# Layer A: the sample's projection first in plain fp32, then the prompt's projection and the sample's attention in one block of static order

## The chip, the cores and the metric

The kernel runs on one core of one Trainium2 chip. TensorE multiplies matrices, VectorE (DVE), ScalarE (ACT) and GpSimd (POOL) do elementwise work, and SyncE (SP) issues most of the loads; DMA engines move data between HBM and the on-chip SBUF. Matmul results land in PSUM banks, from which DVE or ACT copies ("evacuates") them. Every engine runs its own queue of instructions in order, and semaphores tie the queues together. The metric is the device time of one execution in microseconds (us): 3773.86 us as the median of three runs (3769.08 to 3776.07).

## The reference

One step of a two-layer encoder trunk, on 1024 prompt rows (positions 0 to 1023) and on 8 running streams of 16 new rows each (the sample, 128 rows), which attend to 1024 cached keys and values per stream. D_MODEL is 1024, all in fp32. Cut to layer A, which the change touches:

```python
hn = rmsnorm(h, norm_attn[l])
qkv = hn @ w_qkv_a[i]                                # 1024 x 3072
q, k, v = jnp.split(qkv, [A_QK, 2 * A_QK], axis=-1)  # 1024 columns each
q = rope(q.reshape(b, t, 2 * A_HEADS, A_HEAD_DIM), q_pos)
k = rope(k.reshape(b, t, 2 * A_HEADS, A_HEAD_DIM), q_pos)
k_all = concatenate([c_ak, k]);  v_all = concatenate([c_av, v])   # sample only
# diff_attend: two softmax maps per head, 8 heads, values of 128 columns
s = einsum('bqhmd,bkhmd->bhmqk', q, k) * A_HEAD_DIM ** -0.5
p = softmax(where(mask, s, NEG));  w = p[:, :, 0] - lam * p[:, :, 1]
o = einsum('bhqk,bkhe->bqhe', w, v)
h = h + (rmsnorm(o, subln_a) * 0.8) @ w_o_a          # then the MLP, then layer B
```

Outputs are the trunk's rows and the new keys and values of both layers, for prompt and sample.

## The kernel before, in words

The program is a chain of blocks that end in a barrier of all engines: `project_phase` "qkv" (prompt and sample rows together), `prompt_attention` "pa", `decode_attention` "da" (the sample's), `post_phase` "m" (output projection and MLP), and then the same for layer B.

`project_phase` works in 6 pieces of 512 columns (two for Q, two for K, two for V). The weights of a piece come in 4 parts of 512 KB (L201). A float32 product is made of three matmuls in the faster fp32r format (`product`, L144 to L146): every operand is split into a high part (a rounded copy, made by ACT: L438 for weights, L443 for rows) and the rest (`lo`: L240 on POOL for weights, L334 on DVE for rows). A unit is one piece for one row block of 128: 8 times 3 matmuls into a PSUM bank. Nine row blocks (8 prompt, 1 sample) times 6 pieces are 54 units. High and low weights are held for two pieces, so that the next piece is ready when the last ends. DVE evacuates each unit: for Q and K with the rotation, four instructions (L366, L368, L373, L376), for V with one (L360), and ACT's queue issues the store (L459).

`decode_attention` takes the 8 streams one after another. A stream b has 9 steps t, one for each tile of 128 keys (8 cached, one new). In a step TensorE transposes key tile t+1 (`keys`, L1502, 8 transposes into the two banks kb0 and kb1), which ACT (bank 0, L1673) and DVE (bank 1, L1612) evacuate to `kT`; it multiplies tile t with the queries (`scores`, L1520); and for the stream before it works through the probabilities: transposes (`probs`, L1538) and `values` (L1554). ACT makes the exponentials of stream b-1 in steps 0 and 1 of stream b (L1688). At the end, `select` (L1573) gathers the heads' rows. In step 0 TensorE must transpose two key tiles, 0 and 1, into the same two banks, and tile 1 waits until the copies of tile 0 are done. Scores and transposed probabilities have two PSUM banks each; key and value tiles have rings of 4 buffers in SBUF, loaded by SP (L1420, L1425).

The program's waits are on semaphores named in the code; what an engine does next is fixed by the order in which the code writes it. The residual rows `h` are loaded by the qkv block (L205 to L220) and stay in SBUF; `post_phase` adds the output projection to them in `out_add` (L843), after loading attention rows (L569) and weights (L564).

## Time and profile before

| what | value |
|---|---|
| median of three runs | 3773.86 us |
| the profiled execution's own time | 3774.97 us |
| its span, first to last instruction | 3773.3 us |
| mean granted TensorE clock | 0.962 |
| block qkv, from the start to the first load of pa | 0 to 333.4 us |
| block pa, to the first load of da | to 624.3 us |
| block da, to the first load of post_phase | to 855.3 us |
| TensorE busy, whole span | 91% |

All durations below come from the profiled execution. In a table of stretches, a row gives the stretch and its length, then for TensorE (PE), its weight loads (PEld), DVE, ACT and POOL the busy us and the count of instructions in brackets, then the granted TensorE clock as a share of full speed (1.00 is 2.4 GHz, 0.50 is 1.2 GHz), the share of time that the DMA engines were busy, and GB/s. In a timeline, a row gives start, length, engine, line, operation, output<-inputs and shapes; the brackets give how long the engine had been idle before and who ended that. A fp32 matmul is recorded as two rows of weights and two of matmul; an fp32r matmul or a transpose as one.

### The profile page before, as it was taken

The numbers are of one execution on the slowest core, as the hardware profiler recorded it, in microseconds if no ns is written. First come the engines' busy times: TensorE is split into PE (matmuls) and PEld (weight loads), VectorE is DVE, ScalarE is ACT, GpSimd is POOL, SyncE is SP. The second block draws the span as 40 slices with busy tenths as digits, with TensorE's granted clock in tenths as the row PEclk, the third lists the DMA queues.
The fourth block names the chain that finished last, engine by engine and source line by source line (L and its number), as shares of the span: only waits on it lengthen the run. The fifth ranks groups of instructions, "written<-read, shape, count | busy, mean of one in ns | idle before, by whom it ended". The sixth has DMA issues, their size and how long they took to land. (4 is left out here: it accounts for less than half of the span.)

```text
span 3773.3 us, 59284 instructions
## 1 busy us (share of the span) xinstructions
PE 3437.6 (91%) x22922; PEld 2965.5 (79%) x22922; DVE 1697.3 (45%) x2822; ACT 1075.7 (29%) x2054; POOL 478.4 (13%) x188
## 2 busy tenths in 40 slices
PE   7998887887999999999699978868978999999998
PEld 6886776766899999998588867755657899999997
DVE  5423886545444444444312166643432444444445
ACT  3002665333321111112200056642322222221112
POOL 2220000002111111111112100000002111111110
PEclk9998999998999999999889989988988999999999
DMA  4224443973011111110212143427763111111111
GB/s 149 92 85 90 91 100 126 335 285 124 23 45 44 44 44 42 36 44 12 71 59 93 59 100 79 90 57 239 279 214 113 34 45 44 35 43 44 44 50 51
DMA packets 286683, 344.89 MB, mean 91 GB/s; under 512 B 157312, under 2 KB 206496, under 8 KB 286560
## 3 DMA queue, kind: packets, MB, share of 16 engines
q1 hardware_dynamic: 266448, 303.98, 26.1%
q10 hardware_dynamic: 17824, 31.02, 2.3%
q0 software_dynamic: 2304, 8.39, 0.7%
q8 instruction: 76, 1.25, 0.1%
q14 instruction: 31, 0.25, 0.0%
HBM read 299.36 MB, written 43.98 MB: 91 GB/s over the span
## 5 line engine op out<-in xcount | busy, mean ns | idle before, releaser
L879 DVE SCALAR_TENSOR_TENSOR h_rows<-m_dn,m_factor,h_rows 128x512 f32<-128x512 f32 x576 | 429.2, 751 | 311.6 <-PE m_dn L146 311.6
L144 PE MATMUL m_dn<-m_wa,m_wb 128*128 128x512 f32 x1152 | 449.3, 390 | 0.4
L146 PE MATMUL m_dn<-m_wa,m_wb 128*128 128x512 f32 x1152 | 449.0, 390 | 0.0
L145 PE MATMUL m_dn<-m_wa,m_wb 128*128 128x512 f32 x1152 | 448.7, 390 | 0.0
L863 DVE TENSOR_TENSOR m_rows<-m_rows 128x384 f32<-128x384 f32 x192 | 165.5, 862 | 455.2 <-ACT m_rows L754 455.2
L144 PE MATMUL m_up<-b_xt_hi,m_wa 128*128 128x384 f32 x768 | 258.3, 336 | 7.4 <-DVE m_wb L869 4.5
L144 PE MATMUL m_up<-c_xt_hi,m_wa 128*128 128x384 f32 x768 | 257.7, 336 | 7.4 <-DVE m_wb L869 4.5
L145 PE MATMUL m_up<-b_xt_lo,m_wa 128*128 128x384 f32 x768 | 257.8, 336 | 0.0
L146 PE MATMUL m_up<-b_xt_hi,m_wa 128*128 128x384 f32 x768 | 257.7, 336 | 0.0
L146 PE MATMUL m_up<-c_xt_hi,m_wa 128*128 128x384 f32 x768 | 257.5, 335 | 0.0
L145 PE MATMUL m_up<-c_xt_lo,m_wa 128*128 128x384 f32 x768 | 257.3, 335 | 0.0
L144 PEld LDWEIGHTS m_dn<-m_wa,m_wb 128*128 128x128 f32 x1152 | 216.3, 188 | 46.0 <-DVE h_rows L879 2.1
L146 PEld LDWEIGHTS m_dn<-m_wa,m_wb 128*128 128x128 f32 x1152 | 216.2, 188 | 45.2
L145 PEld LDWEIGHTS m_dn<-m_wa,m_wb 128*128 128x128 f32 x1152 | 216.3, 188 | 44.0
L608 POOL TENSOR_TENSOR m_wa<-m_up_raw,m_wa 128x2048 fp32r<-128x2048 f32 x32 | 148.2, 4632 | 744.1 <-ACT m_wa L744 744.1
L749 ACT ACTIVATE m_wa<-m_dn_raw 128x2048 fp32r<-128x2048 f32 x32 | 61.4, 1918 | 632.3 <-PE m_dn L146 632.3
L610 POOL TENSOR_TENSOR m_wa<-m_dn_raw,m_wa 128x2048 fp32r<-128x2048 f32 x32 | 147.2, 4598 | 643.4 <-ACT m_wa L749 643.4
L754 ACT ACTIVATE m_rows<-m_up 128x384 f32<-128x384 f32 x192 | 94.4, 492 | 411.9 <-PE m_up L146 411.9
L144 PE MATMUL kv_acc<-kv_w_hi,b_xt_hi 128*128 128x512 f32 x432 | 173.6, 402 | 24.1 <-POOL kv_w_lo L240 24.1
L144 PE MATMUL qkv_acc<-qkv_w_hi,a_xt_hi 128*128 128x512 f32 x432 | 169.7, 393 | 10.6 <-POOL qkv_w_lo L240 10.6
L146 PE MATMUL kv_acc<-kv_w_hi,b_xt_lo 128*128 128x512 f32 x432 | 172.5, 399 | 0.0
L145 PE MATMUL kv_acc<-kv_w_lo,b_xt_hi 128*128 128x512 f32 x432 | 172.4, 399 | 0.0
(315 smaller groups left out, 6843.5 us busy)
## 6 DMA issues: line engine op xcount, KB each, us to landing
da_k_tiles<-in_cache_a_k SPq DMA_DIRECT2D x64, 512.0 KB, 6.0
da_v_tiles<-in_cache_a_v SPq DMA_DIRECT2D x64, 512.0 KB, 5.4
m_up_raw<-in_w_up SPq DMA_DIRECT2D x32, 1024.0 KB, 5.3
m_dn_raw<-in_w_down SPq DMA_DIRECT2D x32, 1024.0 KB, 4.9
db_k_tiles<-in_cache_b_k SPq DMA_DIRECT2D x64, 512.0 KB, 4.8
db_v_tiles<-in_cache_b_v SPq DMA_DIRECT2D x64, 512.0 KB, 4.5
qkv_w_raw<-in_w_qkv_a SPq DMA_DIRECT2D x24, 512.0 KB, 3.9
m_rows<-o_scratch SPq DMA_DIRECT2D x18, 512.0 KB, 4.0
```

The lines of the kernel that those rows point to most:

```text
L144: pe.matmul(out, lh, rh, start=start, stop=False)
L145: pe.matmul(out, lh, rl, start=False, stop=False)
L146: return pe.matmul(out, ll, rh, start=False, stop=stop)
L608: pool.tensor_tensor(up_lo, up_raw[:], up_hi.bitcast(F32), ALU.subtract).then_inc(s_ul, 1)
L610: pool.tensor_tensor(dn_lo, dn_raw[:], dn_hi.bitcast(F32), ALU.subtract).then_inc(s_dl, 1)
L749: act.activation(dn_hi, dn_raw[:], ACT.Copy).then_inc(s_dh, 1)
L754: act.activation(rl[:, n % 2, :], ups[n % 3][:, 0:GW], ACT.Relu).then_inc(s_ue, 1)
L863: dve.tensor_tensor(rq[:, n % 2, :], rl[:, n % 2, :], rl[:, n % 2, :], ALU.mult).then_inc(s_rq, 1)
L879: dve.scalar_tensor_tensor(hc, dns[n % 3], r2[:, r:r + 1], hc, ALU.mult, ALU.add).then_inc(s_de, 1)
```

## The change

`project_phase` "qkv" and `decode_attention` "da" of layer A are replaced by one block, `project_decode` (tag "da"), and `prompt_attention` runs after it.

First the sample: its 128 rows are transposed and multiplied, unsplit, with the raw fp32 weights of each piece (`sample_unit`, 6 pieces of 8 matmuls), while the prompt's rows are transposed and split. All weights are thus loaded twice, once here and once for the prompt. Then the prompt's 48 units (6 pieces, 8 row blocks) and the decode steps follow one list, `ORDER`, which all engines walk: for each piece four pairs of (convert a quarter of the weights; one decode step), then eight units, each followed by one or two decode steps. The converted weights have room for one piece only. The low part of the weights is now made by DVE with a gain multiply, and the high part by ACT, in calls of 512 columns. The banks for scores and for transposed probabilities are single, the value ring has 3 buffers, and `select` of stream b-2 is in steps 0 and 1 of stream b.

Behind each unit of the first piece and unit 0 of the second stand two steps, behind every other unit one.

The residual rows are no longer loaded by the first block; `post_phase` loads them from the inputs (`load_h`) when `first` is given.

```diff
+def project_decode(nc, core, tag, pieces, gain_src, x, table, lams, k_cache, v_cache, o_rows):
...
+        raw = sb("w_raw", [P, PARTS, KP, HALF])
+        whi, wlo = (sb(f"w_{v}", [P, KT, HALF], F32R) for v in ("hi", "lo"))
...
+        def schedule():
+
+
+
+            steps = [(b, t) for b in range(NB + 1) for t in range(CT + 1)]
+            order, s, units = [], 0, NP * PT
+            for i in range(NP):
+                for j in range(PARTS):
+                    order.append(("weights", i, j))
+                    order.append(("step",) + steps[s])
+                    s += 1
+                for r in range(PT):
+                    order.append(("unit", i, r))
+                    left = (NP - 1 - i) * PARTS
+                    n = -(-(len(steps) - s - left) // (units - i * PT - r))
+                    for _ in range(n):
+                        if s < len(steps):
+                            order.append(("step",) + steps[s])
+                            s += 1
+            return order
...
+            def load_part(n):
+                if n >= PARTS:
+                    if n - PARTS < NS:
+                        sp.wait_ge(s_sw, n - PARTS + 1)
+                    else:
+                        sp.wait_ge(s_wlo, n - PARTS - NS + 1)
+                w, c0 = pieces[n // PARTS % NP][0:2]
+                sp.dma_start(raw[:, n % PARTS], w[:, c0:c0 + HALF].rearrange("(k p) n -> p k n", p=P)[
+                    :, k0_of(n):k0_of(n) + KP, :]).then_inc(s_raw[n % PARTS], 16)
+
+            def load_row(q):
+                if q >= 2:
+                    sp.wait_ge(s_tp, 2 if q == 2 else ROW_EVENT[q - 3] + 2)
+                    sp.wait_ge(s_sq, q - 1)
+                src = x[1] if q == 0 else x[0][(q - 1) * P:q * P, :]
+                sp.dma_start(stage[q % 2], src).then_inc(s_row[q % 2], 16)
...
+                for j in range(PARTS):
+                    load_part(PARTS * (i + 1) + j)
+            load_row(PT)
+            for n in range(KR):
+                load_k(n)
+            for n in range(VR):
+                load_v(n)
+            k, v = KR, VR
+            for kind, a, c in ORDER:
+                if kind == "weights":
+                    if a + 1 < NP:
+                        load_part(NS + PARTS * (a + 1) + c)
+                elif kind == "step":
+                    if c < CT and a < NB:
+                        load_k(k)
+                        k += 1
+                    if a >= 1:
+                        for y in VALUES[c]:
+                            if y < CT:
+                                load_v(v)
+                                v += 1
...
+            def sample_unit(i):
+                if i == 0:
+                    for g in range(2):
+                        pe.wait_ge(s_tf[g], 1)
+                at_least(pe, s_ev, i - 1)
+                for j in range(PARTS):
+                    n = PARTS * i + j
+                    pe.wait_ge(s_raw[j], 16 * (i + 1))
+                    for k in range(KP):
+                        ins = pe.matmul(acc[i % 2][:], xs[:, KP * j + k, :], raw[:, j, k, :],
+                                        start=j == 0 and k == 0, stop=j == PARTS - 1 and k == KP - 1)
+                    ins.then_inc(s_sw, 1)
+
+            def unit(i, r):
+                n = i * PT + r
+                pe.wait_ge(s_ev, NP + n - 1)
+                if i == 0:
+                    e = ROW_EVENT[r] + 1
+                    pe.wait_ge(s_tf[e % 2], e // 2 + 1)
+                    pe.wait_ge(s_tf[1 - e % 2], (e - 1) // 2 + 1)
+                for k in range(KT):
+                    if r == 0 and k % KP == 0:
+                        pe.wait_ge(s_wlo, PARTS * i + k // KP + 1)
+                    lhs = [v[:, k, r * P:(r + 1) * P] for v in (xt_hi, xt_lo)]
+                    ins = product(pe, acc[n % 2][:], lhs, (whi[:, k, :], wlo[:, k, :]), k == 0, k == KT - 1)
+                ins.then_inc(s_mm, 1)
...
+            def step(b, t):
+                if b < NB:
+                    if t == 0:
+                        keys(b, 0)
+                    if t + 1 < CT:
+                        keys(b, t + 1)
+                    scores(b, t)
+                if b >= 2 and t < 2:
+                    select(b - 2, t)
+                if b >= 1:
+                    for v in VALUES[t]:
+                        values(b - 1, v)
+                    for pair in PROBS[t]:
+                        probs(b - 1, pair)
...
+        def evacuation(eng, copy, half):
+
+
+            def keys(b, t):
+                n = b * CT + t
+                eng.wait_ge(s_ktr, 2 * n + half + 1)
+                at_least(eng, s_qk, n - 1)
+                copy(kT[:, t % 2, 4 * half:4 * half + 4, :], KB[half][:]).then_inc(s_ke[half], 1)
...
+            def weight_high(i, j):
+                act.wait_ge(s_raw[j], 16 * (NP + i + 1))
+                at_least(act, s_mm, PT * i)
+                for k in range(KP * j, KP * j + KP):
+                    ins = act.activation(whi[:, k, :], raw[:, j, k % KP, :], ACT.Copy, scale=gcol[:, k:k + 1])
+                ins.then_inc(s_whi, 1)
+
+            def store(i, r):
+                n = i * PT + r
+                dst, d0 = pieces[i][3]
+                act.wait_ge(s_ev, NP + n + 1)
+                act.dma_start(dst[r * P:(r + 1) * P, d0:d0 + HALF], ob[:, n % 2, :]).then_inc(s_st[n % 2], 16)
+
+            def exp(b, g):
+                act.wait_ge(s_nm, b + 1)
+                if b == 0:
+                    act.wait_ge(s_tp, EVENTS)
+                    act.wait_ge(s_sq, RT)
+                at_least(act, s_ptr, 5 * b)
+                at_least(act, s_cf, 2 * b)
+                act.activation(pr[:, g, :], sc[:, g, :], ACT.Exp, bias=nmx[:, g:g + 1],
+                               accum_out=ds[:, g:g + 1]).then_inc(s_e, 1)
...
+            def step(b, t):
+                if b >= 1 and t < 2:
+                    exp(b - 1, t)
+                if b < NB:
+                    if t == 0:
+                        keys(b, 0)
+                    if t + 1 < CT:
+                        keys(b, t + 1)
+                    if t % 2 == 1 or t == CT:
+                        scores(b, t // 2)
+                if b >= 2 and t == 1:
+                    selected(b - 2, 1)
+                    rows_store(b - 2)
+                if b >= 1:
+                    for pair in PROBS[t]:
+                        probs(b - 1, pair)
...
+            for kind, a, c in ORDER:
+                if kind == "weights":
+                    weight_high(a, c)
+                elif kind == "unit":
+                    store(a, c)
+                else:
+                    step(a, c)
...
+            def unit_out(i, r):
+                n = i * PT + r
+                dve.wait_ge(s_mm, n + 1)
+                dve.wait_ge(s_ev, NP + n)
+                if i == 0:
+                    dve.wait_ge(s_rt, r + 2)
+                dve.wait_ge(s_st[n % 2], 16 * (1 + n // 2))
+                rows_out(acc[n % 2][:], r + 1, pieces[i][2], ob[:, n % 2, :], core.cos_sin(r))
+
+            def weight_low(i, j):
+                dve.wait_ge(s_whi, PARTS * i + j + 1)
+                for k in range(KP * j, KP * j + KP):
+                    ins = dve.scalar_tensor_tensor(wlo[:, k, :], raw[:, j, k % KP, :], gcol[:, k:k + 1],
+                                                   whi[:, k, :].bitcast(F32), ALU.mult, ALU.subtract)
+                ins.then_inc(s_wlo, 1)
...
+                factor(i + 1)
+            for kind, a, c in ORDER:
+                if kind == "weights":
+                    weight_low(a, c)
+                elif kind == "unit":
+                    unit_out(a, c)
+                else:
...
+            def load_h(r):
+                if first:
+                    sp.dma_start(h[:, r, :], rows_of(*first[:2], r)).then_inc(s_hr0[r], 16)
...
+                load_h(r - 1)
                 if r + 2 < 2 * PARTS:
                     load_w(r + 2)
+            load_h(RT - 1)
+            if first:
+                for y in range(2):
...
+                if first and p == 0:
+                    dve.wait_ge(s_hr0[r], 16)
...
-        with ExitStack() as rows:
-            core.normed_rows(rows, "a")
-            project_phase(nc, core, "qkv",
-                          [(wa, c, "rope", (*qd, c), 0) for c in (0, HALF)]
-                          + [(wa, D + c, "rope", (kv["ak_p"], kv["ak_s"], c), 0) for c in (0, HALF)]
-                          + [(wa, 2 * D + c, "store", (kv["av_p"], kv["av_s"], c), 0) for c in (0, HALF)],
-                          gains, first=(a["norm_attn"][0, :], a["const"], lams))
+        project_decode(nc, core, "da",
+                       [(wa, c, True, (qd[0], c), (None, c)) for c in (0, HALF)]
+                       + [(wa, D + c, True, (kv["ak_p"], c), (kv["ak_s"], c)) for c in (0, HALF)]
+                       + [(wa, 2 * D + c, False, (kv["av_p"], c), (kv["av_s"], c)) for c in (0, HALF)],
+                       a["norm_attn"][0, :], (xp, xs), a["const"], lams, cak, cav, ao)
+        core.clear_semaphores()
         prompt_attention(nc, core, "pa", False, q, kv["ak_p"], kv["av_p"], None, None, ao)
-        decode_attention(nc, core, "da", False, q[SEQ:ROWS, :], kv["ak_s"], kv["av_s"], cak, cav, None, None, None, ao)
         core.clear_semaphores()
+        core.residual_rows(ctx)
         with ExitStack() as rows:
             core.normed_rows(rows, "b")
             post_phase(nc, core, "m0", ao, a["w_o_a"].rearrange("n d e -> (n d) e"), a["subln_a"][0, :],
-                       a["w_up"][0], a["w_down"][0], a["norm_mlp"][0, :])
+                       a["w_up"][0], a["w_down"][0], a["norm_mlp"][0, :], (xp, xs, gains))
```

How the change orders TensorE at the start of the program: before, the fp32r units begin right behind the first transposes (`turn` is the bank of transposed rows, `acc` a unit's bank).

```order
L251 MATMUL qkv_turn<-const_sb,qkv_xn 128x128 x16
L144 MATMUL qkv_acc<-qkv_w_hi,a_xt_hi 128x512
L145 MATMUL qkv_acc<-qkv_w_lo,a_xt_hi 128x512
L146 MATMUL qkv_acc<-qkv_w_hi,a_xt_lo 128x512
L144 MATMUL qkv_acc<-qkv_w_hi,a_xt_hi 128x512
```

After, on the same engine at the same place (`xs_T` holds the sample's rows, `probs` is the buffer in which raw rows are staged, `out_rows` a finished piece of the sample):

```order
L702 MATMUL da_kb<-const_sb,da_probs 128x128 x8
L723 MATMUL da_acc<-da_w_raw,da_xs_T 128x512 x8
L702 MATMUL da_kb<-const_sb,da_probs 128x128 x8
L723 MATMUL da_acc<-da_w_raw,da_xs_T 128x512 x8
L702 MATMUL da_kb<-const_sb,da_out_rows 128x128 x4
L702 MATMUL da_kb<-const_sb,da_probs 128x128 x8
L723 MATMUL da_acc<-da_w_raw,da_xs_T 128x512 x8
```

Six such fp32 groups, with all row transposes, now stand ahead of the first decode step and the first prompt unit.

Step 0 of a stream on ACT, before: the copy of key tile 0 stands ahead of the exponential (line 1688), the copy of tile 1 behind it. The rows without a tile are register work and waits.

```order
L1673 ACTIVATE da_kT<-da_kb 128x512
L1686 ISA
L1687 ISA
L1688 ACTIVATE da_probs,da_sum<-da_scores,da_neg_max 128x1152
L1610 REGISTER_ALU
L1611 REGISTER_ALU
L1673 ACTIVATE da_kT<-da_kb 128x512
```

After, step 0 of stream 3, behind unit 2 of the second piece, on ACT (`q_scratch<-da_out_rows` is the store of a unit, which waits until DVE has evacuated it):

```order
L926 DMA q_scratch<-da_out_rows 128x512
L935 ACTIVATE da_probs,da_sum<-da_scores,da_neg_max 128x1152
L882 ACTIVATE da_kT<-da_kb 128x512 x2
L926 DMA q_scratch<-da_out_rows 128x512
L935 ACTIVATE da_probs,da_sum<-da_scores,da_neg_max 128x1152
```

The unit's store and the exponential now stand ahead of both key copies of the step.

The boundary between the second and the third piece on DVE. Before, DVE had no weights to convert there, only unit after unit:

```order
L366 SCALAR_TENSOR_TENSOR qkv_times_cos<-qkv_acc,row_factor,const_sb 128x512
L368 SCALAR_TENSOR_TENSOR qkv_times_sin<-qkv_acc,row_factor,const_sb 128x512
L373 TENSOR_TENSOR qkv_out_rows<-qkv_times_cos,qkv_times_sin 128x8x32
L376 TENSOR_TENSOR qkv_out_rows<-qkv_times_cos,qkv_times_sin 128x8x32
L366 SCALAR_TENSOR_TENSOR qkv_times_cos<-qkv_acc,row_factor,const_sb 128x512
```

After, on DVE (line 1050 ends the evacuation of the second piece's last unit, `w_lo` are the weights' low parts, `kT` the key copies):

```order
L1050 TENSOR_TENSOR da_out_rows<-da_out_rows,da_times_sin 128x8x32
L848 COPY da_kT<-da_kb 128x512
L1100 TENSOR_REDUCE da_max<-da_scores 128x2
L1075 SCALAR_TENSOR_TENSOR da_w_lo<-da_w_raw,da_gain_column,da_w_hi 128x512 x2
L848 COPY da_kT<-da_kb 128x512
L870 COPY da_probs_T<-da_pb 128x256
L1075 SCALAR_TENSOR_TENSOR da_w_lo<-da_w_raw,da_gain_column,da_w_hi 128x512 x2
L861 COPY da_scores<-da_sb 128x2x128 x2
L1100 TENSOR_REDUCE da_max<-da_scores 128x2
L1075 SCALAR_TENSOR_TENSOR da_w_lo<-da_w_raw,da_gain_column,da_w_hi 128x512 x2
```

Between two units there now stand the weights' low parts, each ahead of the next step's copies.

## Rows read from the trace of the kernel before

**Rows 1.** The page's head.
```profile
span 3773.3 us, 59284 instructions
```
**Rows 2.** Table of stretches, cut at the three blocks of layer A.
```profile
0.00:333.40 333.40, 306.41 (x1368) 253.49 (x1368) 122.66 (x215) 49.16 (x73) 58.82 (x29) 1.00 0.29 100
333.40:624.30 290.90, 238.61 (x1632) 210.18 (x1632) 226.91 (x448) 175.80 (x416) 7.75 (x10) 0.93 0.42 87
624.30:855.30 231.00, 190.60 (x3136) 149.21 (x3136) 103.72 (x192) 89.18 (x180) 4.94 (x17) 0.95 0.83 300
```
**Rows 3.** Stretches: start-up, the units behind it, and seven streams of da.
```profile
0.00:27.00 27.00, 3.91 (x16) 3.14 (x16) 7.14 (x11) 11.23 (x15) 10.86 (x8) 1.00 0.71 253
27.00:331.00 304.00, 302.50 (x1352) 250.35 (x1352) 114.84 (x200) 36.69 (x57) 47.95 (x20) 1.00 0.25 86
...
660.00:848.00 188.00, 162.34 (x2790) 127.98 (x2792) 88.70 (x165) 73.96 (x150) 3.48 (x12) 0.97 0.86 312
```
**Rows 4.** Stretch of the middle of da.
```profile
660.00:748.00 88.00, 79.31 (x1412) 63.69 (x1414) 44.87 (x82) 36.37 (x74) 1.74 (x6) 1.00 0.91 333
```
**Rows 5.** Timeline of TensorE, the first unit: slow matmuls, then fast ones.
```profile
27.64 0.63 PE L145 MATMUL qkv_acc<-qkv_w_lo,a_xt_hi 128*128 128x512 f32 x1
28.06 0.63 PE L146 MATMUL qkv_acc<-qkv_w_hi,a_xt_lo 128*128 128x512 f32 x1
...
32.03 0.39 PE L145 MATMUL qkv_acc<-qkv_w_lo,a_xt_hi 128*128 128x512 f32 x1
32.26 0.40 PE L146 MATMUL qkv_acc<-qkv_w_hi,a_xt_lo 128*128 128x512 f32 x1
```
**Rows 6.** Timeline of da, step 0 of a stream, and its select.
```profile
726.55 1.64 PEld L1573 LDWEIGHTS da_pb<-da_o_diag,const_sb 128*16 128x16 f32 x16 [1.18 <-ACT da_o_diag L1680]
...
728.40 0.85 PEld L1502 LDWEIGHTS da_kb<-const_sb,da_k_tiles 128*128 128x128 f32 x8 [0.21 <-issue]
...
730.09 0.60 ACT L1673 ACTIVATE da_kT<-da_kb 128x512 f32<-128x512 f32 x1 [0.91 <-PE da_kb L1502]
730.59 1.25 ACT L1688 ACTIVATE da_probs<-da_scores,da_neg_max 128x1152 f32<-128x1152 f32 x1
730.74 0.86 PEld L1502 LDWEIGHTS da_kb<-const_sb,da_k_tiles 128*128 128x128 f32 x8 [1.48 <-ACT da_kT L1673]
```
**Rows 7.** Timeline of da, TensorE: a step with values, scores to scores.
```profile
742.66 0.38 PEld L1520 LDWEIGHTS da_sb<-da_kT,da_q_diag 128*32 128x32 f32 x16 [0.17 <-issue]
...
745.56 0.38 PEld L1520 LDWEIGHTS da_sb<-da_kT,da_q_diag 128*32 128x32 f32 x16 [0.17 <-issue]
```
**Rows 8.** A unit's evacuation on DVE: ns minimum, median and maximum, and when.
```profile
L366 DVE SCALAR_TENSOR_TENSOR qkv_times_cos<-qkv_acc,row_factor,const_sb x36: 750/751/752, 34.8 to 231.7; 128x512 f32<-128x512 f32 x36
L368 DVE SCALAR_TENSOR_TENSOR qkv_times_sin<-qkv_acc,row_factor,const_sb x36: 741/743/743, 35.4 to 232.4; 128x512 f32<-128x512 f32 x36
L360 DVE TENSOR_SCALAR qkv_out_rows<-qkv_acc,row_factor x18: 750/751/751, 237.1 to 329.6; 128x512 f32<-128x512 f32 x18
```
**Rows 9.** The same evacuation's third instruction.
```profile
L373 DVE TENSOR_TENSOR qkv_out_rows<-qkv_times_cos,qkv_times_sin x36: 424/425/1149, 36.2 to 233.1; 128x256 f32<-128x256 f32 x36
```
**Rows 10.** Groups of 660 to 848 us: key copies, busy us, mean ns, idle before.
```profile
L1612 DVE COPY da_kT<-da_kb 128x512 f32<-128x512 f32 x52 | 36.0, 691 | 37.4 <-PE da_kb L1502 37.4
...
L1673 ACT ACTIVATE da_kT<-da_kb 128x512 f32<-128x512 f32 x52 | 30.9, 594 | 32.6 <-PE da_kb L1502 32.4
```
**Rows 11.** The page's DMA issues: KB each, median us to landing.
```profile
da_k_tiles<-in_cache_a_k SPq DMA_DIRECT2D x64, 512.0 KB, 6.0
da_v_tiles<-in_cache_a_v SPq DMA_DIRECT2D x64, 512.0 KB, 5.4
...
qkv_w_raw<-in_w_qkv_a SPq DMA_DIRECT2D x24, 512.0 KB, 3.9
```
**Rows 12.** Timeline: the first transposes of da, and its last store.
```profile
632.04 3.59 PE L1482 MATMUL da_kb<-const_sb,da_new_rows 128*128 128x128 f32 x16 [13.27 <-DMA da_new_rows<-out_ak_s]
...
851.98 0.33 ACTq L1702 DMA_DIRECT2D o_scratch<-da_o_out  x1
```

418 lines of the change are left out of this document (415 added, 3 removed).

## The prediction

> **What bounds the kernel now.** I read the page's head first (the whole span) [rows 1], then the table of stretches cut at the barriers of layer A. The three blocks take 333.4, 290.9 and 231.0 us [rows 2]. Only the first and the third are rewritten, 564.4 us together. In the first, TensorE is busy for 302.5 of 304.0 us behind a start-up of 27 us [rows 3]: it is bound by TensorE's pace. Two fp32r matmuls start 0.23 us apart at full clock [rows 5]. The 54 units and the transposes fill 27 to 329.6 us; with 72 transposes at 0.11 (0.85 us for eight [rows 6]), which is 8, and 2 us for the slow start, a unit is (302.6 - 10)/54 = 5.42, and I use 5.44 us. In the third, TensorE is busy for 162.3 of the 188 us of seven streams, 26.9 us a stream, with the DMA engines at 0.86 [rows 3]. The timeline tells which steps wait. A step with values goes from scores to scores in 2.90 us [rows 7], filled to the 0.2 us turns between kinds of matmul: it can't be hidden, only moved. Step 0 waits: TensorE transposes key tile 0 at 728.40 and tile 1 only at 730.74, 1.48 us of it on ACT's copy [rows 6]. The idle part is 25.7/7 = 3.7 us a stream; by adding the turns back differently it is up to 4.9. So a stream is 22.0 to 23.2 us of TensorE work, I take 22.5, and da is 180 us of work in 231. The 51 us of rest (13.3 us before the first transposes [rows 12], the last stream's values alone, the 3.7 a stream) are all that interleaving can recover.
>
> **The change part by part** (us; durations from the profiled execution, 3774.97 us, which is 1.1 above the median of the runs).
>
> *Removed:* 54 units and both blocks: 564.4.
>
> *Sample phase.* An fp32 matmul of 128 columns takes 1.64/8 = 0.205 (sixteen weight rows) [rows 6], so one of 512 columns four times that, 0.82 to 0.85, and a piece 8 x 0.85 = 6.8, against 5.44 as a unit. Start: in the first 27 us loads move 253 GB/s [rows 3], so the sample rows are there at about 6.5, turned and scaled at 10, and piece 0 runs for its first 4 us at the slow level (0.42 between matmuls [rows 5]): it ends at 19. Each further piece has 6.8, eight transposes (0.9), four for the new Q and K (0.45), and the wait for ACT to free their bank (0.6 copy [rows 10], and its turn): 9.1. Pieces 1 to 4 and the last: 66.
>
> *Transition.* The last prompt row's load waits in SP's queue behind all sample weights and lands 8 later; transpose, high part, square and root take until +12. Then four pairs of weight conversion and step run in lockstep: DVE has 2 x 0.75 for the low part [rows 8], 0.69 for its key copy [rows 10], and maxima, some 3.3 a pair, and TensorE needs that copy before the next pair. Unit 0 starts at 66 + 23.5, plus 2.5 for the slow clock behind such gaps: 92. The row for a TensorE without work before 27 us [rows 3] is the bound from below (start of units at 75), 105 the one above.
>
> *Units and steps.* 48 x 5.44 = 261. Steps 180, less the 7 that lie in the transition: 173.
>
> *Step 0 of streams 1 to 7.* Behind a rotated unit, ACT first waits for the evacuation, 0.2 + 0.75 + 0.74 + 0.42 + 0.42 = 2.55 [rows 8, 9], issues the store (3.0), makes the exponential (1.25 + 0.19, to 4.4) and only then copies key tile 0 (5.0). TensorE had finished its transpose at 0.9 and waits 4.1 for the bank; behind that wait stand its scores, the select and the next unit. Behind an unrotated unit it is 2.5. Seven times: 24. Before, that wait was 1.48 [rows 6] and is in the 231.
>
> *Two steps behind a unit* (nine times): the second one's transposes need ACT's copy, at 3.5 for the same reason, and find TensorE ready after 1.4 (no values), 2.5 or 2.9: 0.6 to 2.1 each, 3.5 with an exponential: 12.
>
> *Piece boundaries.* DVE has the last unit's 2.35, five steps' copies and four low parts of 1.5; TensorE has five steps of 22.5/9, 12.5, and can start the next unit after about 16.5. Five times 4: 20. Before, two pieces of weights were held and this was nothing. If all steps there were light it could be 2, with exponentials 7.
>
> *Value tiles.* A tile takes 5.4 to land [rows 11]; a ring of three with two tiles used in a step of 2.9 starves where such steps follow each other without a unit between (four boundaries and three double steps): 1.5 to 3 each, partly under DVE's wait: 10, bounds 0 and 25.
>
> *Tail.* Last outputs, select, copy and store: 8. Afterwards one more barrier, 1; residual rows reloaded in a stretch with spare DMA, queued behind the attention rows they could delay: 1.
>
> Sum: 92 + 261 + 173 + 24 + 12 + 20 + 10 + 8 = 600, and 2 behind it; before 564.4. The difference is +37, on 3774.97 it is 3812, and against the median 3811. I take 3810.
>
> A row and a rule on the clock: in the middle of da, two fifths of whose TensorE work is transposes (82 a stream, 0.11 each [rows 6], of 22.5), the granted clock is 1.00, the level of 2.4 GHz, after unbroken work before it [rows 4]. The Trainium skill (TensorE: Matmul & The Clock Gate, Part 4: PE-mode transpose) says that transposes do not engage the full clock, as they don't count as busy in the same way. By that rule the sample phase and the steps would slow down in the new block; by the row they don't, and the sum has nothing for it.
>
> **The rivals.**
>
> *A. TensorE's waits are covered, and it gets faster.* For it: between two units every copy has 5.44 us to finish, ACT and DVE are busy for 74 and 89 of 188 us in da [rows 3], and key loads run three steps ahead. If sample phase and transition stay as computed and the waits (24 + 12 + 20 + 10) come to 15 in all, the block is 549 and the time 3775 - 15 + 2 = 3762; with a start of units at 75, 3745. Against it: the list fixes that store and exponential stand ahead of the copies.
>
> *B. The sample phase is bound by loads.* A loop moves four weight parts and a row, 2.6 MB; at 9.1 us that is 288 GB/s. For it: the start-up moved 253 [rows 3], at which a loop is 10.4 and the phase 7 longer: 3818. At a load's landing of 6 us [rows 11] behind its issue, the margin is only half a us. Against it: 333 GB/s were moved with tiles of the same 512 KB [rows 4]. The Trainium skill (DMA: Bandwidth & Descriptors, Bandwidth) asks for DMAs of at least 1 MiB for 75% of peak; its rule would make parts of 512 KB the bound of this phase. The row with several such tiles in flight speaks against it here.
>
> *C. The single banks and the short value ring decide.* All 20 or so heavy steps without a unit between take 4.3 instead of 2.9 (a ring of three per 5.4 + 0.9), and boundaries cost 8: 3810 + 28 = 3838. For it: the boundaries behind pieces 2 and 4 fall into value steps. Against it: landing is faster (3.9 [rows 11]) with less traffic.
>
> *D. It cancels:* gain of the interleaving and price of the sample phase within 7 us: 3774. For it: both are some 50 us, and my sum is a small difference.
>
> **How the numbers follow.** Forecast (3792 to 3828) 0.45, A 0.20, B 0.14, C 0.13, D 0.08. A difference below 0.2%, 7.5 us, can't be told from none. Faster comes from A: 0.20; same from D and the edge of A: 0.09; slower from the rest: 0.71. The forecast's own range is 3792 to 3828; to leave out no more than 0.2, with half of A inside and C up to its price, it becomes 3760 to 3842.
>
> **What would show it.** The first fp32r matmul of a unit at 85 to 100 us (below 80 the sample phase or the transition is oversized); fp32 matmul rows for the sample about 0.43 us apart; the block's end at 590 to 612; at each step 0, TensorE's transposes of tile 1 waiting 4 us on ACT's copy, and the ACT row of the exponential ahead of it; at piece boundaries about 16 us without an fp32r matmul; TensorE's busy time in the block about 440. The forecast is wrong if those waits are under 20 us together, if the units are spread (a unit over 5.6), or if the block of the prompt's attention changes from 291, which I hold constant.

## The result and the profile after

The changed kernel takes 3835.27 us (median of four, 3834.61 to 3838.08), the kernel before 3773.24 us beside it: a ratio of 1.016 with a 95% interval of 1.0148 to 1.0172. It is slower by 62 us, 25 more than the forecast of 3810. That is inside the stated range of 3760 to 3842, but 7 us outside the forecast's own 3792 to 3828. The profiled execution took 3834.74 us. First the page's head and the table of stretches of the changed kernel, in the columns of [rows 2]. The cuts are the end of the sample's pieces, the first prompt unit, the first load of the prompt's attention (pa) and that of the post phase:

```profile
span 3832.8 us, 58469 instructions
```
```profile
0.00:66.00 66.00, 54.43 (x169) 27.72 (x170) 21.62 (x52) 22.27 (x40) 1.28 (x7) 1.00 0.88 297
66.00:90.20 24.20, 13.86 (x120) 10.19 (x119) 12.56 (x24) 13.79 (x28) 0.00 (x0) 0.72 0.88 318
90.20:621.60 531.40, 462.38 (x4172) 367.20 (x4168) 206.97 (x372) 108.38 (x210) 5.30 (x14) 0.94 0.47 161
621.60:913.30 291.70, 237.24 (x1632) 210.09 (x1632) 226.73 (x448) 175.82 (x416) 7.76 (x10) 0.94 0.40 87
```

The new block ends at 621.6; the two it replaces took 564.4 [rows 2], so 57.2 are lost inside it. The prompt's attention takes 291.7 instead of 290.9, and all behind it 1.5 more (2919.5 us of the span against 2918.0). That is 59.5, the whole difference of the spans [rows 1]. Nothing went wrong elsewhere.

The third row is the one to read. From the first unit to the end, TensorE has 462.4 us of work and is idle for 69.0, and the granted clock is 0.94. The gaps and the clock go together, as will be seen.

The start came as forecast. TensorE in the sample phase (start, length, line): a piece of eight fp32 matmuls, recorded as 16 rows 0.43 apart, takes 7.0, and the pieces follow each other at 8.7 (30.84, 39.56). Then the last prompt row's transposes wait 5.6 for its load:

```profile
30.84 7.11 PE L723 MATMUL da_acc<-da_w_raw,da_xs_T 128*128 128x512 f32 x16 [1.17 <-DMA da_w_raw<-in_w_qkv_a]
...
39.56 7.03 PE L723 MATMUL da_acc<-da_w_raw,da_xs_T 128*128 128x512 f32 x16
...
72.63 1.97 PE L702 MATMUL da_kb<-const_sb,da_probs 128*128 128x128 f32 x8 [5.58 <-DMA da_probs<-in_x_prompt]
```

What TensorE waits for behind the first unit (us in total, times, longest), changed kernel:

```profile
PE da_kb L749 <- ACT da_kT L882: 37.2, 15, 4.4
PE da_ob L793 <- DMA da_v_tiles<-in_cache_a_v: 14.8, 9, 4.6
PE da_kb L749 <- DVE da_kT L848: 3.2, 4, 1.2
```

The largest is the step-0 wait, which [rows 6] show at 1.48. The timeline of one of them, behind a rotated unit of the fourth piece (step 0 of stream 6, with the exponentials of stream 5):

```profile
432.60 1.03 PE L749 MATMUL da_kb<-const_sb,da_k_tiles 128*128 128x128 f32 x8
...
435.16 0.34 ACTq L926 DMA_DIRECT2D out_ak_p<-da_out_rows  x1
435.62 1.25 ACT L935 ACTIVATE da_probs<-da_scores,da_neg_max 128x1152 f32<-128x1152 f32 x1 [6.16 <-DVE da_out_rows L1050]
...
436.88 0.58 ACT L882 ACTIVATE da_kT<-da_kb 128x512 f32<-128x512 f32 x1
...
437.60 1.94 PE L749 MATMUL da_kb<-const_sb,da_k_tiles 128*128 128x128 f32 x8 [3.96 <-ACT da_kT L882]
...
439.47 1.08 PE L764 MATMUL da_sb<-da_kT,da_q_diag 128*32 128x128 f32 x16
```

Read it from the right: TensorE finished tile 0's transposes at 433.6 and gets the bank back at 437.6. ACT had been idle for 6.16 us, in its queue behind DVE's rotation, because the unit's store stands ahead of the step; then store, exponential, and only then the copy. And the eight transposes behind the wait take 1.94 instead of 1.03, the sixteen score matmuls 1.08 instead of 0.64: the clock fell to 1.2 GHz in the gap, as the row of the stretch behind it shows (0.50). A wait of 4 costs over 5.

```profile
437.60:442.10 4.50, 4.50 (x32) 3.33 (x32) 0.69 (x1) 0.60 (x1) 0.00 (x0) 0.50 0.31 108
```

Key and value tiles land about as long behind their issue as before, weight parts 1.1 later [rows 11]; the weights are converted in calls of 719 ns on ACT:

```profile
da_k_tiles<-in_cache_a_k SPq DMA_DIRECT2D x64, 512.0 KB, 5.4
da_v_tiles<-in_cache_a_v SPq DMA_DIRECT2D x64, 512.0 KB, 5.5
...
da_w_raw<-in_w_qkv_a SPq DMA_DIRECT2D x48, 512.0 KB, 5.0
```
```profile
L919 ACT ACTIVATE da_w_hi<-da_w_raw,da_gain_column 128x512 fp32r<-128x512 f32 x40 | 26.4, 719 | 0.9 <-ACT da_xs_T L882 0.9
```

### The profile page after: what moved, and what is told of

It is laid out like the page before. It is cut to its first block and busy times, and to the rows that moved or that the text cites. A ratio compares the mean times of both kernels' runs of the same rounds, so it can differ in the third digit from the quotient of the medians.

```text
span 3832.8 us, 58469 instructions
## 1 busy us (share of the span) xinstructions
PE 3470.3 (91%) x22874; PEld 2968.3 (77%) x22874; DVE 1711.1 (45%) x2861; ACT 1081.6 (28%) x2078; POOL 421.3 (11%) x164
## 5 line engine op out<-in xcount | busy, mean ns | idle before, releaser
L363 DVE TENSOR_SCALAR kv_out_rows<-kv_acc,row_factor 128x512 f32<-128x512 f32 x54 | 40.5, 750 | 269.6 <-PE kv_acc L149 269.6
```

The lines of the kernel that those rows point to most:

```text
L363: dve.tensor_scalar(o, src_, rstd[:, r:r + 1], None, ALU.mult).then_inc(s_ev, 1)
```

## The experiments

Twelve kernels, all made from the changed one. Each is timed against the kernel before on its own chip, where the latter's median was 3774.7 to 3776.5 (3773.2 beside the changed kernel); differences of 1 to 3 us between two kernels of the table can come from that alone. "Stretch" is from the first prompt unit to the first load of pa; idle is its length less TensorE's busy time.

| run | median us | ratio to before (95%) | stretch | busy | idle |
|---|---|---|---|---|---|
| changed kernel | 3835.3 | 1.0148 to 1.0172 | 531.4 | 462.3 | 69.0 |
| e_actorder | 3805.6 | 1.0064 to 1.0091 | 499.2 | 451.7 | 47.5 |
| e_allorder | 3802.2 | 1.0055 to 1.0083 | 496.4 | 453.0 | 43.5 |
| e_doubles_late | 3827.2 | 1.0121 to 1.0152 | 520.0 | 457.0 | 63.0 |
| e_sequential | 3845.8 | 1.0165 to 1.0197 | - | - | - |
| e_order_ring | 3795.2 | 1.0038 to 1.0062 | 489.8 | 453.9 | 36.0 |
| e_lowpool | 3836.8 | 1.0142 to 1.0181 | 526.6 | 460.3 | 66.4 |
| e_best | 3796.9 | 1.0039 to 1.0065 | 486.0 | 449.6 | 36.4 |
| e_flush | 3779.8 | 1.0007 to 1.0024 | 471.8 | 441.8 | 30.1 |
| e_two | 3771.6 | 0.9986 to 1.0004 | 466.5 | 446.1 | 20.5 |
| e_none | 3775.9 | 0.9995 to 1.0012 | 467.0 | 443.0 | 23.9 |
| e_single_last | 3769.2 | 0.9972 to 0.9990 | 464.5 | 444.4 | 20.2 |
| e_stage | 3769.7 | 0.9979 to 0.9997 | 463.0 | 443.4 | 19.6 |

**e_actorder.**

```diff
@@ ScalarE
             def step(b, t):
+                if b < NB and t == 0:
+                    keys(b, 0)
                 if b >= 1 and t < 2:
                     exp(b - 1, t)
                 if b < NB:
-                    if t == 0:
-                        keys(b, 0)
...
+            waiting = []
             for kind, a, c in ORDER:
+                if kind != "step" and waiting:
+                    store(*waiting.pop())
...
-                    store(a, c)
+                    waiting.append((a, c))
```

> ScalarE only: in step 0 of a sequence the copy of key tile 0 stands ahead of the previous sequence's exponential, and the store of a prompt unit stands behind the steps that follow the unit. Theory (the order on ScalarE holds TensorE at step 0): of the 37.2 us that TensorE waits for a key copy of ScalarE, about half goes, since VectorE's own scores and unit copy come at nearly the same time; the block ends 10 to 20 us earlier, 3815 to 3825 us. Rival 1 (single banks of kb, sb, pb and the short ring of value tiles decide): within 4 us of the changed kernel, 3831 to 3839. Rival 2 (the slow clock behind each gap is the price): gaps get shorter, so the loss at the half clock falls as well and the gain is above 20 us, under 3815.

Measured: 30 us less, more than the theory's 10 to 20 and under 3815, as rival 2 said. The same place in its timeline, and its stretch:

```profile
410.70 1.03 PE L749 MATMUL da_kb<-const_sb,da_k_tiles 128*128 128x128 f32 x8
...
411.33 0.60 ACT L882 ACTIVATE da_kT<-da_kb 128x512 f32<-128x512 f32 x1 [5.03 <-PE da_kb L749]
...
411.83 1.25 ACT L935 ACTIVATE da_probs<-da_scores,da_neg_max 128x1152 f32<-128x1152 f32 x1
...
413.88 0.66 PE L749 MATMUL da_kb<-const_sb,da_k_tiles 128*128 128x128 f32 x4 [1.18 <-DVE da_kT L848]
414.47 0.64 PE L764 MATMUL da_sb<-da_kT,da_q_diag 128*32 128x128 f32 x16
```
```profile
88.77:587.99 499.22, 451.73 (x4172) 359.00 (x4168) 205.74 (x372) 110.52 (x210) 5.33 (x14) 0.97 0.51 171
```

The copy now stands ahead of the exponential and doesn't wait for the store, and what is late next is DVE's copy behind the rotation. From the first transpose to the scores it is 3.8 us against 6.9. The stretch is 32.2 shorter: 21.5 of it is idle time and 10.6 is busy time of the same 4172 recorded matmuls, which ran at a clock of 0.97 and not 0.94. So both explanations hold, two thirds to one third. The store was moved behind every unit, and not only where a step 0 follows, so the 32.2 spread: 14.0 come at the four steps 0 between units of a piece, 6.5 at the doubles, 4.8 at the boundaries, 3.2 in the units themselves and 3.7 behind the last unit.

**e_allorder.** As e_actorder, with the same `waiting` list around `unit_out` on DVE.

> The same, and on VectorE the rotation and copy of a unit's output stands behind the steps as well. Theory: both halves of a key tile are now copied before anything else is done at step 0 and behind a unit; waits at steps 0 and at doubles (34 us above the plain steps) fall to under 10, so 3800 to 3812 us. Rival 1 (single banks, ring): 3829 to 3839. Rival 3 (the unit's bank comes free too late, since acc is only double): the units that follow a double step wait for acc, and the time is that of e_actorder or up to 10 us more.

Measured: 3802, within the theory's interval, but only 3 less than e_actorder, which the intervals do not separate, and where some 14 had been expected between them. Its waits:

```profile
PE da_kb L749 <- ACT da_kT L882: 15.4, 10, 4.9
PE da_ob L793 <- DMA da_v_tiles<-in_cache_a_v: 14.7, 9, 4.3
```

The wait on ACT's copy, 8.2 in e_actorder, is back at 15.4, longest 4.9. The doubles of piece 0 gained (the gaps between its units fell from 35.0 to 29.2), while boundaries 3 and 4 grew from 18.7 and 25.0 to 23.7 and 28.0. Why is seen in e_flush.

**e_doubles_late.** `n` in the list is rounded down instead of up, so that two-step places come last.

> The two-step places stand at the last eight units instead of the first ones. Theory: the eight doubles of the first piece cost 20 us above plain steps, because the evacuations of two steps and a unit's rotation meet there; the last piece's units are value units that are not rotated, so the same doubles are cheaper by 8 to 12 us there, 3823 to 3828 us. Rival (the key stream bounds the doubles, one key tile in 3.2 us at most from the pool of queues): the same time, 3831 to 3839, since the stream's waits move with them.

Measured: 8 less, 3827, as the theory said. The waits on ACT's copy fell from 37.2 to 30.9, those for value tiles rose from 14.8 to 19.0:

```profile
PE da_kb L749 <- ACT da_kT L882: 30.9, 11, 5.2
PE da_ob L793 <- DMA da_v_tiles<-in_cache_a_v: 19.0, 10, 3.3
```

**e_sequential.**

```diff
                 for j in range(PARTS):
                     order.append(("weights", i, j))
-                    order.append(("step",) + steps[s])
...
+            order += [("step",) + y for y in steps]
```

> All 48 prompt units first, then all 81 decode steps: nothing is interleaved, the sample phase stays in front. Theory (interleaving does hide the loads of K and V, but the added sample phase of 90 us and the waits eat it up): 90 to the first unit, 48 units of 5.6 and five boundaries of about 9 without cover, 314, then the stream alone as before the change, 231 less the part of it that started early, and the block ends near 635 to 650: 3850 to 3865 us. Rival (the interleaving costs more in waits and slow clock than it hides): the block ends under 615 and the time is under 3828.

Measured: 3846, 11 above the changed kernel, 4 below the theory's interval and far from the rival's. So interleaving, as the changed kernel does it, is worth only 11 us (8 by the ratios). Its three stretches (start, 48 units, 81 steps), from an execution that was 6 us slower than the median of its four:

```profile
0.00:79.80 79.80, 57.19 (x184) 29.85 (x185) 27.13 (x65) 30.69 (x57) 1.28 (x7) 0.94 0.90 313
79.80:380.60 300.80, 273.52 (x1153) 224.00 (x1154) 114.38 (x189) 27.17 (x44) 0.00 (x0) 0.94 0.22 77
380.60:635.60 255.00, 202.98 (x3121) 157.63 (x3119) 104.53 (x193) 89.90 (x177) 4.09 (x14) 0.89 0.74 254
```

A unit takes 5.44 where units follow each other, and a boundary without steps stands still for 5.9 and slows the next unit by 1.8. The steps alone need 255, 24 more than da before [rows 2]: TensorE waits 25.6 for value tiles there.

**e_order_ring.** e_allorder with `KR, VR = 3, 4` in place of `4, 3`.

> Both orders (ScalarE and VectorE) as in e_allorder, and rings of 3 key tiles and 4 value tiles in place of 4 and 3, in the same memory. Theory (the third value tile is the shortage at boundaries and doubles, where steps stand close): of the 14.7 us that TensorE waits for value tiles in the block of e_allorder, 10 or more go and fewer than 4 come back as waits for key tiles: 3788 to 3795 us. Rival (the transfers share their queues with four weight parts of 512 KB each at the boundary, and land late whenever they are issued): the value waits stay above 10 us and the time at 3798 to 3806.

Measured: 7 less, 3795.2, at the theory's upper edge; the stretch is 6.6 shorter. The value waits are gone, and a little more than the theory allowed (4.9, not under 4) came as waits for key tiles:

```profile
PE da_kb L749 <- ACT da_kT L882: 14.5, 9, 4.9
...
PE da_kb L749 <- DMA da_k_tiles<-in_cache_a_k: 4.9, 5, 1.8
...
PE da_ob L793 <- DMA da_v_tiles<-in_cache_a_v: 1.1, 2, 0.6
```

**e_lowpool.**

```diff
+                    dve.tensor_tensor(gained[:, 4 * g:4 * g + 4, :], KB[e % 2][:],
+                                      gcol[:, 4 * g:4 * g + 4].unsqueeze(2).to_broadcast([P, 4, P]),
+                                      ALU.mult).then_inc(s_gr, 1)
...
-                for k in range(KP * j, KP * j + KP):
-                    ins = act.activation(whi[:, k, :], raw[:, j, k % KP, :], ACT.Copy, scale=gcol[:, k:k + 1])
+                act.activation(whi[:, KP * j:KP * j + KP, :], raw[:, j], ACT.Copy).then_inc(s_whi, 1)
...
+                    pool.tensor_tensor(wlo[:, KP * c:KP * c + KP, :], raw[:, c], whi[:, KP * c:KP * c + KP, :].bitcast(F32),
+                                       ALU.subtract).then_inc(s_wlo, 1)
```

> From the changed kernel: the gain is multiplied into the prompt's turned rows once (VectorE, 16 products of 128x512 in the sample phase), so a weight part's high half is one ScalarE copy of 128x1024 and its low half is one subtraction on GpSimd instead of two on VectorE. Theory (the casts of the weights stretch the boundary's four steps on both evacuating engines, 49 us above plain steps over five boundaries): VectorE is freed of 2.8 us and ScalarE of 0.3 us per part, and the boundaries lose 10 to 20 us, against 0 to 3 us more in the sample phase: 3817 to 3828 us. Rival 1 (value tiles bound the boundaries): 3832 to 3838. Rival 2 (the subtraction takes GpSimd over 3 us a part, and the fourth part comes after the fourth step): boundaries grow by up to 3 us each, 3838 to 3855.

Measured: no difference, 3837. Theory fallen, the time is rival 1's: the gaps at the boundaries add up to 107 us against 111, and the waits on ACT's copy and for value tiles are 36.1 and 16.4, as before. The theory had also doubled what a part costs DVE: 2.8 was said, two calls take 1.41. Rival 1's reason, that value tiles bound the boundaries, is not shown by this run; e_order_ring is the one that tests it. A low half takes 2369 ns on GpSimd:

```profile
L707 POOL TENSOR_TENSOR da_w_lo<-da_w_raw,da_w_hi 128x1024 fp32r<-128x1024 f32 x22 | 52.1, 2369 | 183.8 <-ACT da_w_hi L937 182.9
```

**e_best.** e_order_ring, e_doubles_late and e_lowpool together.

> All together: both orders, doubles in the last piece, rings of 3 and 4, gain on the rows and the low halves on GpSimd. If the terms add (orders -33, doubles -8, ring -10, casts -10) the block ends about 60 us before the changed kernel's and the time is 3770 to 3785 us, the kernel before; if they overlap (the same boundaries paid for once only) 3786 to 3798. Under 3765 only if the clock stays at its upper level through the boundaries as well.

Measured: 3796.9, no better than e_order_ring: the overlap case. With the orders mended, doubles cost the same early or late (gaps of pieces 0 and 5 together 37.8 against 35.5), and the ring of three key tiles now waits 15.0.

**e_flush.** e_order_ring, but both `waiting` lists are emptied only ahead of the next unit:

```diff
-                if kind != "step" and waiting:
+                if kind == "unit" and waiting:
```

> As e_order_ring, but the output of a piece's last unit is rotated, copied and stored behind the four weight casts and steps of the boundary, just ahead of the next unit. Theory (at boundaries 3 and 4 the rotation and copy, moved behind the steps for good everywhere else, now stands ahead of the first weight cast: 24.2 and 21.7 us there against 18.7 in the changed order of ScalarE alone): the boundaries lose 2 to 3 us each, 3782 to 3790 us. Rival (the four steps' own evacuations bound the boundary): 3792 to 3798.

Measured: 3779.8, 15 less than e_order_ring and better than the theory's interval. Boundary 3 in e_order_ring, timeline of DVE and ACT, then TensorE:

```profile
339.01 0.42 DVE L1055 TENSOR_TENSOR da_out_rows<-da_out_rows,da_times_sin 128x256 f32<-128x256 f32 x1
...
339.91 1.33 ACT L919 ACTIVATE da_w_hi<-da_w_raw,da_gain_column 128x512 fp32r<-128x512 f32 x2 [2.89 <-DVE da_out_rows L1055]
341.15 0.57 ACT L882 ACTIVATE da_kT<-da_kb 128x512 f32<-128x512 f32 x1
...
341.86 1.08 PE L749 MATMUL da_kb<-const_sb,da_k_tiles 128*128 128x128 f32 x4 [4.90 <-ACT da_kT L882]
```

and in e_flush, the same instruction:

```profile
330.02 0.63 PE L749 MATMUL da_kb<-const_sb,da_k_tiles 128*128 128x128 f32 x4 [1.91 <-ACT da_kT L882]
...
332.08 1.08 PE L764 MATMUL da_sb<-da_kT,da_q_diag 128*32 128x128 f32 x16
332.94 1.91 PE L804 MATMUL da_pb<-da_o_diag,const_sb 128*16 128x128 f32 x8
```

ACT stood 2.89 us in front of the store, with the cast and the key copy behind it. This is the same queue as at step 0, and it stood at all five boundaries, with a step 0 in them or not: each became 2 to 4 us shorter, 14.6 together. This is counted from e_order_ring; e_allorder had made the boundaries 8.5 longer than they were in e_actorder, so a part of it is taken back from there. Last, the wait of 1.91 (and one of 0.85 behind it) is not free either: the transposes right behind it are fast, but the scores and the select that follow take 1.08 and 1.91 instead of 0.64 and 1.04, at half the clock. The first row below is that place, the second the whole stretch, whose clock rose to 0.99 (0.96 before):

```profile
332.00:335.00 3.00, 3.00 (x27) 2.02 (x26) 0.80 (x2) 2.05 (x4) 0.00 (x0) 0.51 0.88 284
88.77:560.60 471.83, 441.77 (x4172) 354.29 (x4168) 206.53 (x371) 111.12 (x210) 4.22 (x14) 0.99 0.52 181
```

**e_two.** e_flush with steps behind the second and the fourth weight part only, at boundaries 1 to 5:

```diff
+            AT = ((0, 1, 2, 3), (1, 3))
...
-                    order.append(("step",) + steps[s])
-                    s += 1
+                    if j % 4 in AT[i > 0]:
+                        order.append(("step",) + steps[s])
+                        s += 1
```

> As e_flush, with two steps at each boundary behind the first (ahead of the second and the fourth weight part's) instead of four; the ten steps that this frees stand as doubles behind units, 17 doubles in all. Theory (a step between two casts costs about 5 us, since the casts' engines also evacuate it, and one beside another step behind a unit about 3): 10 steps save 1.5 to 2 us each: 3768 to 3780 us. Rival 1 (the boundary's waits are the step's own: evacuation of key tiles at 3 us a step, wherever it stands): the time of e_flush within 4 us. Rival 2 (the transfers of K and V bound the doubled stretches): above e_flush by 5 or more.

**e_none.** The same with `AT = ((0, 1, 2, 3), ())`.

> As e_flush, with no step at the five boundaries behind the first; 27 doubles. In e_sequential such a boundary stood 5.9 us and made the next unit 1.8 us longer. Theory: 20 steps behind units at about 3 us each in place of the boundaries' 20 to 24 us each: 7.7 + 12 = 20 against 21 to 24, so 3765 to 3785 us, and near e_two. Rival (TensorE idles with nothing to cover the cast, and the doubled steps wait): 3790 to 3805.

Measured: 3771.6 and 3775.9; both theories hold, and both kernels are level with the kernel before. e_two idles 9.6 us less than e_flush, yet its work takes 4.3 more at a lower clock:

```profile
90.36:556.88 466.52, 446.05 (x4172) 358.91 (x4168) 206.36 (x370) 111.24 (x210) 4.75 (x14) 0.98 0.53 182
```

In e_none, TensorE waits for the low half where nothing covers it:

```profile
PE da_acc L147 <- DVE da_w_lo L1082: 15.9, 5, 4.0
```

**e_single_last.**

```diff
-                    left = (NP - 1 - i) * len(AT[1])
-                    n = -(-(len(steps) - s - left) // (units - i * PT - r))
+                    left = (NP - 1 - i) * len(AT[1]) + NP - i
+                    n = -(-(len(steps) - s - left) // ((NP - i) * (PT - 1) - r)) if r < PT - 1 else 1
```

> As e_two, but the last unit of a piece is never followed by two steps, so that three steps and not four stand between two pieces at boundaries 1 and 2 (16.2 us each in e_two, where boundaries 3 and 4 with three steps stand 10.1 and 8.5 us); the two steps go behind units, at about 3 us each. Theory (a step at a boundary costs the time of its evacuation on engines that also cast): 2 x (16.2 - 9.3 - 2.9) = 8 us less: 3761 to 3766 us. Rival (boundaries 1 and 2 are long for another reason, the full stream of K and V at doubles and weights): within 3 us of e_two, 3769 to 3775.

Measured: 3769.2, 2 to 3 less than e_two and not 8. That is inside the rival's interval. Against the kernel before, each on its own chip, it is 5 us less than e_two (0.9981 and 0.9995), with intervals that overlap. Boundary 1 fell from 16.2 to 9.5, as computed, but boundary 2 only to 14.3, and other doubles moved: the unit behind boundary 1 is now followed by 9.1 us instead of 5.7. So boundary 1 behaved as the theory says, and the rest of its gain did not come. The stretch:

```profile
90.24:554.78 464.54, 444.38 (x4172) 357.65 (x4168) 206.33 (x371) 111.07 (x210) 4.48 (x14) 0.98 0.54 184
```

This is the version that beats both kernels: 0.9981 of the kernel before (0.9972 to 0.9990), 66 us below the changed one, with the same engines, memory and loads. Against the kernel before the gain is at the edge of what can be told; e_stage beside it has 0.9988.

**e_stage.** e_single_last with `stage = [pr[:, 0, 0:D], pr[:, 1, 0:D], sc[:, 1, 0:D]]` and `load_row(PT)` ahead of the last four `load_part`.

> As e_single_last, and a third tile for the staged rows (in the scores, unused there), so that the last prompt row's load is issued ahead of the last four weight parts and not when the row before the last but one is turned. Theory (TensorE waits 4.8 us for that row, from 66.3 to 71.1 us): 3 to 5 us less than e_single_last, first unit at 85 to 87 us: 3757 to 3762. Rival (behind the row the first key tiles and weight parts bound the start, which the row only hides): first unit at 89 to 91 us and the time of e_single_last.

Measured: 3769.7 against 3769.2, the same. The start came as the theory said, the time did not. In the profile the last row's wait is gone and the first unit starts at 86.8 instead of 90.2, but the key tiles behind it now are late:

```profile
66.50 1.16 PE L705 MATMUL da_kb<-const_sb,da_scores 128*128 128x128 f32 x8 [2.10 <-DVE da_xt_lo L1032]
69.33 1.94 PE L752 MATMUL da_kb<-const_sb,da_k_tiles 128*128 128x128 f32 x8 [1.67 <-DMA da_k_tiles<-in_cache_a_k]
...
80.66 1.09 PE L752 MATMUL da_kb<-const_sb,da_k_tiles 128*128 128x128 f32 x8 [1.84 <-DMA da_k_tiles<-in_cache_a_k]
```

This profiled execution is the fastest of its eleven, and the medians don't confirm its 5 us. What the start would give is left open.

## Why the prediction was right, and where it was 25 us short

The sign, the place and most terms were right; the block was taken 21.6 too short, and 3810 was rounded down from 3812. The result is above the forecast's own 3792 to 3828 and falls in the stated range only because that had been widened up to the price of rival C, whose reasons mostly did not hold. Two of the prediction's signs failed as well: the block's end was to be at 590 to 612 (621.6), and TensorE's busy time about 440 (462.3 from the first unit on). The terms, with measured values (gaps are from the end of a unit's last matmul to the start of the next unit's first; a plain step leaves 1.5 to 2.8):

| step of the prediction | said | measured |
|---|---|---|
| first unit starts | 92 | 90.2 |
| 48 units | 261 | 273.7 |
| steps outside the transition, without waits | 173 | 164 |
| waits at steps 0, doubles, boundaries, for value tiles | 24 + 12 + 20 + 10 = 66 | 83 |
| tail | 8 | 10.5 |
| block | 600 | 621.6 |
| behind the block | 2 | 2.3 |

**Start: right.** A piece at 8.7 instead of 9.1, the transition 24.2 instead of 26. Rival B (loads bind the sample phase at 10.4 a piece) is wrong: 297 GB/s, with 1.2 us of wait for a weight part at most in the rows above. Parts of 512 KB kept the DMA engines at 0.88 and moved 297 to 318 GB/s. The Trainium skill (DMA: Bandwidth & Descriptors, Bandwidth) asks for 1 MiB a transfer for 75% of peak; by an estimate from the 436 GB/s that the page has as the peak, these rates are 68 to 73% of it and don't contradict the rule. What they show is that such parts were fast enough for this phase; [rows 4] moved 333.

**Units: mis-sized, 12.7 of the 21.6.** The prediction took 5.44, measured where units follow each other, and e_sequential has just that. Between steps a unit is 5.57, as its first matmul stands 0.33 ahead of the second instead of 0.23 and the kinds of matmul alternate: 48 x 0.13 = 6. The other 6.4 are seven units that began at 1.2 GHz, up to 7.57. The text itself named a unit over 5.6 as a sign that it is wrong, and the mean is 5.70.

**Plain steps: 9 too long.** 164 were measured where 173 were said; this error hid 9 us of the others.

**Step 0: right in mechanism and in size.** 4.1 was said behind a rotated unit, 3.96 is measured, in the said order of store, exponential, copy. TensorE's waits on ACT's copy in the seven steps 0 are 4.05, 3.96, 3.96, 3.14, 4.40, 3.96 and 2.41, 25.9 where 24 was said. The first, third, sixth and seventh stand between two units of a piece and cost 18.6 above a plain step 0, slow transposes behind the wait included, where 4/7 of 24 is 14; the other three (streams 2, 4 and 5) lie at boundaries 1 to 3. That the order on ACT decides was shown by e_actorder, which moves those two calls alone and takes back 30 of 62, 14 of them at these four places.

**Doubles: 15 besides the share of step 0, where 12 were said.** Right within its size.

**Boundaries and value tiles: mis-sized, 49.3 and not 30.** I counted DVE's work (2.35 + casts + copies) against TensorE's, and gave 4 each. Measured are 18.0, 6.4, 8.5, 12.6 and 3.8 above plain steps. They hold four things. Steps 0 of three streams, with 11.5 us of waits at boundaries 1 to 3, had been priced in the 24 above. The store and the rotation stand ahead of the casts and the copies, and the ring is too short by one value tile: from the changed kernel to e_flush, which mends both, the gaps at the boundaries fall from 111 to 92 us (the ring by itself, in e_order_ring: 14.7 of waits become 1.1, 7 us of time). And the steps are dearer there than behind a unit (e_two: 8 us). DVE's casts, the reason I had given, were not the bound: e_lowpool moved them to GpSimd and gained nothing, though TensorE waits for none of them there. What else stands in the 92 is open.

**The clock: missing from the sum.** This is the step that was wrong in kind, since the sum had 2.5 for the slow clock, at the start, and nothing behind the gaps that it forecast. TensorE's work in the stretch takes 462.3 at a mean clock of 0.94 and 441.8 at 0.99 (e_flush), with the same 4172 recorded matmuls: 20 us. These are in the table's units and waits already. The prediction looked at [rows 4], a stretch without gaps, and asked only whether transposes slow the clock. They don't: e_flush has as many transposes as the changed kernel and a clock of 0.99; what differs is TensorE's idle time, 30 against 69. The amount of idle time isn't all: e_two idles 20 at a clock of 0.98 and needs 446.1. Whether the rest is the length of the single gaps or what stands around them, no run here separates. The Trainium skill (TensorE: Matmul & The Clock Gate, Part 4: PE-mode transpose) says that transposes do not engage the full clock; for transposes that stand among other matmuls these stretches speak against it, and no run here has them alone. The same rows show what I should have asked: what a gap costs beyond its own length.

**The rivals.** A (waits covered, 3762) was excluded by the list alone: with another list and other orders, e_single_last is at 3769, and its idle time of 20 us holds the tail too, so that A's 15 of waits were about reached. C gave 3838, nearest to the time, but for other reasons: its sum is 28 us for heavy steps, and its dearer boundaries aren't in it; the single banks cost nothing that shows, since steps without an exponential leave the plain 1.5 to 2.8 us (no kernel with double banks was run); of C only the ring is real. D (both cancel) is what e_two to e_stage show, once the waits are gone: the overlap of attention and projection gives back what the sample phase of 90 us costs, and 7 us more. That this phase itself costs that much is read from the trace and was not tested by a kernel without it.

## What to carry to other kernels

When two phases are merged into one static order, write down per engine what stands ahead of the one instruction that frees a bank: here a store and an exponential put 4 us of queue ahead of a copy of 0.6, and moving these two calls gave back half of the loss. Put what nobody waits for (stores, the rotation of a finished unit) behind what the bottleneck waits for, and check the same at places where the pattern breaks, such as the boundary of a piece. And price a gap in front of TensorE with the slow clock behind it: from the changed kernel to e_actorder 21.5 us of idle time took 10.6 of busy time along. The share is no constant: from e_order_ring to e_flush it was 12.1 of busy time with 5.9 of idle, from e_flush to e_two none.

## What the runs showed of the hardware

- Work of TensorE was 20 us longer for the same instructions when its idle time rose from 30 to 69 us in 470 to 530 (e_flush and the changed kernel). The eight transposes behind a wait of 3.96 took 1.94 instead of 1.03. Behind a wait of 1.18 everything stayed fast (e_actorder). Behind one of 1.91, with 0.85 after it, the transposes stayed fast and the next matmuls ran at 1.2 GHz (e_flush); in e_stage eight transposes took 1.94 behind 1.67, and 1.09 behind 1.84. The length of the last wait alone does not tell.
- The low half of a weight part (128x1024, fp32r out) takes 2.37 us on GpSimd, and two calls on DVE with the gain in them 1.41 (timeline of e_order_ring, 341.27 us). ACT's cast of 128x512 with a scale per partition takes 719 ns, a plain copy of that size from PSUM 592.
- An fp32 matmul of 512 columns is two records 0.43 apart, 0.86 together, nearly four fp32r matmuls of 0.23 at the same clock.
